# State stores of a two-layer streaming encoder: rows instead of columns, two heads per DMA

## What is computed

```
C_new = decay[..., None, None] * C + jnp.einsum('bhs,bhsd,bhse->bhde', ws, k, v)
n_new = decay[..., None] * n + jnp.einsum('bhs,bhsd->bhd', ws, k)
...
qs = rope(wq.reshape(B, S, SW_HEADS, SW_DH), pos)
ks = rope(wk.reshape(B, S, SW_KV, SW_DH), pos)
new_k, new_v = ks[:, -WINDOW:], vs[:, -WINDOW:]
```

## Time and profile before

| | us |
|---|---|
| median of 3 runs (lowest 2055.12, highest 2057.03) | 2056.2 |
| the profiled execution's own time | 2051.92 |
| its span | 2049.8 |
| TensorE busy in the span | 1999.7 |
| VectorE busy | 1242.4 |
| ScalarE busy | 781.3 |
| GpSimd busy | 945.1 |

### The profile page before, as it was taken

How to read it: one execution, slowest core, us unless ns; L and a number is a source line. 1 busy time by engine, 2 the same in 40 slices (tenths; PEclk the granted TensorE clock), 3 DMA queues, 4 the chain that set the end, 5 groups by cost and what they waited for, 6 DMA issues and landing times.

```text
span 2049.8 us, 39052 instructions
## 1 busy us (share of the span) xinstructions
PE 1999.7 (98%) x15897; PEld 1924.1 (94%) x15897; DVE 1242.4 (61%) x1993; ACT 781.3 (38%) x1672; POOL 945.1 (46%) x532
## 2 busy tenths in 40 slices
PE   8998999999999999999999899999999999999998
PEld 7997898899999999999999889989999999999997
DVE  5564787466647535647567557863765573647473
ACT  4243334223334333425533343342244343525253
POOL 0421244565673646364734212545748446364543
PEclk9998999999999999999999989999999999999999
DMA  9844233123351332323544332332233413232332
GB/s 360 308 135 47 61 104 108 55 73 93 99 188 34 128 126 86 93 83 103 176 167 156 67 55 72 87 104 70 73 93 124 134 46 89 83 91 84 94 93 78
DMA packets 301314, 221.41 MB, mean 108 GB/s; under 512 B 14752, under 2 KB 294864, under 8 KB 297424
## 3 DMA queue, kind: packets, MB, share of 16 engines
q1 hardware_dynamic: 294384, 215.38, 34.9%
q10 hardware_dynamic: 6752, 3.53, 0.7%
HBM read 209.37 MB, written 8.79 MB: 106 GB/s over the span
## 4 chain that ended last, share of the span: by engine, by line
PE 87%; DMA 4%; DVE 3%; POOL 2%; issue 2%; ACT 1%; SPq 0%; DVEq 0%; ACTq 0%; POOLq 0%
PE ps L1196 23%; PE ps L1297 19%; PE ps L1224 14%; PE ps L1664 9%; PE ps L1992 5%; DMA raw<-in_w_in 3%; PE ps L1317 3%; PE ps L1323 2%; PE ps L1450 2%; PE ps L1365 1%; PE ps L1892 1%; PE ps L1855 1%; PE ps L1717 1%; PE ps L1870 1%; PE ps L1732 1%
## 5 line engine op out<-in xcount | busy, mean ns | idle before, releaser
L1123 POOL TENSOR_TENSOR a_lo<-raw,a_hi 128x512 fp32r<-128x512 f32 x108 | 159.3, 1476 | 275.3 <-ACT a_hi L2682 275.3
L1079 POOL TENSOR_TENSOR hi_lo<-raw,consts 128x1024 fp32r<-128x1024 f32 x70 | 141.7, 2025 | 253.5 <-PE ps L1196 153.0
L1196 PE MATMUL ps<-h_hi,hi_lo 128*128 128x288 f32 x1216 | 218.6, 298 | 0.0
L1099 POOL TENSOR_TENSOR hi_lo<-raw,hi_lo 128x512 fp32r<-128x512 f32 x60 | 80.4, 1342 | 292.5 <-ACT hi_lo L2258 292.2
L1196 PEld LDWEIGHTS ps<-h_hi,hi_lo 128*128 128x128 f32 x1216 | 180.0, 189 | 4.4 <-issue 3.2
L1082 POOL TENSOR_TENSOR hi_lo<-raw,hi_lo 128x1024 fp32r<-128x1024 f32 x70 | 177.9, 2541 | 5.5
L1224 PE MATMUL ps<-yf_hi,fo_h 128*128 128x288 f32 x704 | 152.2, 298 | 0.9 <-DVE yf_lo L2857 0.9
L1224 PE MATMUL ps<-yf_hi,fo_l 128*128 128x288 f32 x704 | 150.9, 296 | 0.0
L1224 PE MATMUL ps<-yf_lo,fo_h 128*128 128x288 f32 x704 | 150.8, 296 | 0.0
L1196 PE MATMUL ps<-h_lo,hi_lo 128*128 128x288 f32 x608 | 130.0, 295 | 0.0
L1079 POOL TENSOR_TENSOR hx<-raw,consts 128x1024 fp32r<-128x1024 f32 x28 | 55.6, 1985 | 147.4 <-PE ps L1323 65.0
(11 more groups left out here) (509 smaller groups left out, 6141.4 us busy)
## 6 DMA issues: line engine op xcount, KB each, us to landing
ada<-in_w_ada SPq DMA_DIRECT2D x23, 2048.0 KB, 9.1
raw<-in_w_ffn_in SPq DMA_DIRECT2D x144, 256.0 KB, 3.1
raw<-in_w_in SPq DMA_DIRECT2D x120, 256.0 KB, 3.3
raw<-in_w_in SPq DMA_DIRECT2D x48, 512.0 KB, 3.7
raw<-in_w_ffn_out SPq DMA_DIRECT2D x32, 384.0 KB, 3.3
raw<-in_w_ffn_out SPq DMA_DIRECT2D x32, 320.0 KB, 3.1
raw<-in_w_out SPq DMA_DIRECT2D x16, 512.0 KB, 3.6
raw<-in_w_ffn_in SPq DMA_DIRECT2D x16, 512.0 KB, 3.8
```

What stands on the lines that cost most here:

```text
L1079: pool.tensor_tensor(hi, RAW[s][:, 0:size], ONES[:, 0:1].to_broadcast([128, size]), ALU.mult).then_inc(chunk_hi, 1)
L1099: pool.tensor_tensor(lo, RAWB[o], hi.bitcast(f32), ALU.subtract).then_inc(h_alo, 1)
L1123: pool.tensor_tensor(lo[:, :], RAWB[o], hi[:, :].bitcast(f32), ALU.subtract).then_inc(s_alo, 1)
L1196: m = pe.matmul(o[:, h, :], a[:, k, c0:c0 + 128], mv(k, h), start=(k == 0 and begins), stop=(k == nk - 1 and a is wl))
```

## The change

It has three parts.

**State stores.** `n` is no longer stored as a column. In the turn of head 1, inside `back(0)`, TensorE transposes the 129th columns of the four heads (prompt, then sample: two transposes of 128x4) into free columns of the PSUM unit of `back(0)`, after a wait for head 3's state. In `gate_head(0)` VectorE copies the 4x256 values to `NROWS`, four partitions of the tile KOUT, which is free then, and ScalarE's queue stores them with two DMAs of four rows of 512 bytes (`store_rows`). `C` is stored for two heads by one DMA (`store_states`): heads 0 and 1 where they were, heads 2 and 3 together behind `after_p2(3)`. In all 8 DMAs in place of 18 per layer.

**Order on VectorE.** `rope_sine(1)` stands ahead of `after_p5(8)` (`h_weights(4, 8)` and `h_weights_low(3, 8)`), not behind it.

**Last keys.** The two copies from unit `ko` to KOUT are done by ScalarE, right ahead of the stores, and no longer by VectorE ahead of `after_p7(8)`.

```diff
@@ -322,7 +322,7 @@
 
 
 VROW_DMAS, PARAM_DMAS = 5, 10
-C_STORES, O_STORES = 18, 5
+C_STORES, O_STORES = 8, 5
 
 
 def build(nc, A, O, XD):
@@ -478,6 +478,7 @@
         QK, SU, YTK = MID, MO, KW
         KA, KB = KALL[:, 1, :], KALL[:, 0, :]
         STG, GT = KOUT, SQ
+        NROWS = KOUT[0:4, :, :]
         ADA_BUF = [ADA[:, 0, :], ADA[:, 1, :], ADA2[:, :], ADA3[:, :],
                    MID[:, :, :].rearrange("p k c -> p (k c)")[:, 0:4096]]
         SV = VT[:, :, :, :].rearrange("p t h c -> p (t h c)")[:, 0:2560].rearrange("p (t c) -> p t c", t=5)
@@ -675,7 +676,7 @@
         gh_ready = event("gh_ready", 22)
         gl_ready = event("gl_ready", 22, 2)
         zb_ready = event("zb_ready", 4)
-        c_stored, o_stored, ln_loaded = sem("c_stored"), sem("o_stored"), sem("ln_loaded")
+        c_stored, o_stored, ln_loaded, n_rows = sem("c_stored"), sem("o_stored"), sem("ln_loaded"), sem("n_rows")
 
         def done_by(name):
 
@@ -1743,6 +1744,10 @@
                         pe.wait_ge(unit_of(l, _b(h)[0][0]), read(l, _b(h)[0][0]))
                     for t in range(NTT):
                         pe.transpose(unit(l, nm)[:, t * 128:(t + 1) * 128], YTK[:, t, :], IDN)
+                    if h == 0:
+                        pe.wait_ge(unit_of(l, "cm3"), read(l, "cm3"))
+                        for j in range(2):
+                            pe.transpose(unit(l, nm)[0:4, 640 + j * 128:768 + j * 128], COUT[:, :, j, 128], IDN)
                     pe.transpose(unit(l, nm)[:, 512:576], YTK[0:64, 4, :], IDN[0:64, 0:64]).then_inc(done_by(nm), 1)
 
                 def row_columns():
@@ -2362,13 +2367,17 @@
                     act.dma_start(O[nm][ds(l, 1)].rearrange("l b (h o) -> (l b h) o", o=1), IG[:, c:c + 1]) \
                        .then_inc(c_stored, 16)
 
-                def store_state(h):
-                    act.wait_ge(unit_of(l, f"cm{h}"), read(l, f"cm{h}"))
+                def store_states(h):
+                    act.wait_ge(unit_of(l, f"cm{h + 1}"), read(l, f"cm{h + 1}"))
                     for j, w in enumerate(("prompt", "sample")):
-                        act.dma_start(O[f"C_{w}"][ds(l, 1), 0, h].rearrange("l d e -> (l d) e"), COUT[:, h, j, 0:128]) \
-                           .then_inc(c_stored, 16)
-                        act.dma_start(O[f"n_{w}"][ds(l, 1), 0, h].rearrange("l (d o) -> (l d) o", o=1),
-                                      COUT[:, h, j, 128:129]).then_inc(c_stored, 16)
+                        act.dma_start(O[f"C_{w}"][ds(l, 1), 0, h:h + 2].rearrange("l h d e -> (l d) h e"),
+                                      COUT[:, h:h + 2, j, 0:128]).then_inc(c_stored, 16)
+
+                def store_rows():
+                    act.wait_ge(n_rows, l + 1)
+                    for j, w in enumerate(("prompt", "sample")):
+                        act.dma_start(O[f"n_{w}"][ds(l, 1), 0].rearrange("l h d -> (l h) d"),
+                                      NROWS[:, j, :]).then_inc(c_stored, 16)
 
                 def decay(h):
 
@@ -2406,12 +2415,10 @@
                 after_p5(2)
                 after_p6(2)
                 after_p2(2)
-                store_state(0)
-                store_state(1)
+                store_states(0)
                 after_p7(2)
                 after_p3(2)
                 after_p4(2)
-                store_state(2)
                 for h in range(4):
                     h_keep(0, 3 + h)
                     decay(h)
@@ -2422,7 +2429,9 @@
                     after_p6(3 + h)
                     after_p2(3 + h)
                     if h == 0:
-                        store_state(3)
+                        store_states(2)
+                    elif h == 1:
+                        store_rows()
                     elif h == 2:
                         act.wait_ge(c_stored, l * (16 * C_STORES) + 16 * C_STORES)
                     after_p7(3 + h)
@@ -2449,6 +2458,9 @@
                 after_p5(8)
                 after_p6(8)
                 after_p2(8)
+                act.wait_ge(done_by("ko"), done(l, "ko"))
+                act.activation(KOUT[:, 0, :], unit(l, "ko")[:, 0:128], ACT.Copy)
+                act.activation(KOUT[0:64, 1, :], unit(l, "ko")[0:64, 128:256], ACT.Copy).then_inc(unit_of(l, "ko"), 1)
                 act.wait_ge(unit_of(l, "ko"), read(l, "ko"))
                 for nm, src in (("k_prompt", KOUT[:, 0, :]), ("k_sample", KOUT[0:64, 1, :]),
                                 ("v_prompt", VSW[:, NTT - 1, :]), ("v_sample", VSW[0:64, NTT, :])):
@@ -3394,6 +3406,8 @@
                     nm = _b(h)[1][0]
                     dve.wait_ge(done_by(nm), done(l, nm))
                     h_second_done(dve, l, 2 + h // 2)
+                    if h == 0:
+                        dve.tensor_copy(NROWS, unit(l, nm)[0:4, 640:896].rearrange("p (j c) -> p j c", j=2)).then_inc(n_rows, 1)
                     dve.scalar_tensor_tensor(YT[:, :], MO[:, h, :], 1.0, unit(l, nm)[:, 0:T], ALU.add, ALU.mult).then_inc(unit_of(l, nm), 1)
 
                 def y_lo(i, src):
@@ -3461,13 +3475,10 @@
                 after_p4(7)
                 rope_sum(0)
                 after_p1(8)
+                rope_sine(1)
                 after_p5(8)
-                rope_sine(1)
                 after_p6(8)
                 rope_sum(1)
-                dve.wait_ge(done_by("ko"), done(l, "ko"))
-                dve.tensor_copy(KOUT[:, 0, :], unit(l, "ko")[:, 0:128]).then_inc(dve_step, step())
-                dve.tensor_copy(KOUT[0:64, 1, :], unit(l, "ko")[0:64, 128:256]).then_inc(unit_of(l, "ko"), 1)
                 after_p7(8)
                 after_p3(8)
                 after_p4(8)
```

## The result

The changed kernel takes 2023.26 us (median of 4 runs, 2022.69 to 2023.65) against 2055.66 us before (4 runs, 2054.33 to 2057.03): 32.4 us less, ratio 0.9842 with a 95% interval of 0.9825 to 0.9859. The forecast was 25.2 us less, 2031.0 us, with 2027 as the lower end of its range. The direction and the place were right, the gain was larger than the range allowed. The profiled execution of after took 2023.58 us; that of before had taken 2051.92.

The account below looks back on a forecast made before the run. TensorE, busy 98% of the span, was held by loads slowed behind 4-byte `n` writes. Stop and clock 24.8, minus transposes 0.6, plus rotary part 1.0, gave 25.2 us less: 2031.0 us, range 2027 to 2044.

Parts of the forecast that it names:

- the 7.9 us stop: TensorE's wait at L1697, head 3's state, traced to a load slowed by 4-byte `n` writes; 7.2 us a layer would go.
- Rivals (a) to (c): Load behind head 0/1 stores: `C` shares blame, 2046.6 (0.10); `C` or bank alone, 2055.8 (0.05); pairing `C` slows, 2061.6 (0.03).
- 5.2 us a layer: Time lost to TensorE's half clock from head 3's state to head 0's scores, expected to go with the stop.
- TensorE's new work: Two added transposes of `n` on TensorE, taken as 0.3 us a layer, 0.6 us in all.
- VectorE's copy: Added copy of 4x256 values from PSUM, at most 0.68 us and some 0.4 us, expected to add nothing.
- The two waits of the rotary part: TensorE's 0.5 us for `rope_sine` and 0.7 us for `h_half(8)`; 0.5 us a layer gained together, 1.0 in all.
- the median of the runs stands 4.3 us above that execution, so it would be 2056.2 - 25.2: Step from the profiled execution, 2051.92 us, to the forecast median, 2031.0 us, keeping the offset unchanged.
- I take 3.9 us: Expected duration of the load issued at 156.53 beside 256 KB of `C` rows, instead of 11.14 us.
- The 0.7 us of stop: Part of TensorE's wait at head 3's state expected to stay in each layer, keys being ready at 163.8.
- 24.8 - 0.6: Both layers' gain from stop and clock, 12.4 us each, less the cost of TensorE's added transposes.
- The range: 8 in 10 range for the changed kernel, 2027 to 2044 us; the likeliest case alone spanned 2028 to 2036.
- The two rules: Below 512 bytes a transfer becomes a read-modify-write; or a small packet costs a few cycles and 32 bytes, nearly free.

Follow-up runs that it names:

- `rows_only`: Kernel before with only `n` stored as rows through transposes, `C` still per head and the rotary part as before: 2024.30 us, ratio 0.9854.
- `no_n`: Kernel before with the `n` stores left out, `C` stores as before: 2025.90 us, ratio 0.9846.
- `no_c`: Kernel before with the `C` stores left out, `n` still stored as columns: 2074.51 us, ratio 1.0084.
- `before_again`: Kernel before, unchanged, with clock and span of every run: 2055.02 us over 12 runs.
- `rotary_only`: Kernel before with only `rope_sine(1)` moved earlier and the last keys copied by ScalarE: 2053.36 us, ratio 0.9989.
- `n_step64`: Kernel before with the `n` column elements written 64 bytes apart into the prompt output, `n` itself not stored: 2024.42 us, ratio 0.9863.
- `pairs_only`: Kernel before with only `C` stored in pairs of heads at the change's places, `n` still in 4-byte columns: 2035.04 us, ratio 0.9905.

## Why the prediction was right in the place and wrong in the size

**Right.** The chain's step from the 7.9 us stop to the load behind the stores, and from there to the 4-byte writes, not the `C` rows, carried: `rows_only` and `no_n` get nearly all of the gain. Rivals (a) to (c) are out with them; `no_c` goes further, since it has no `C` rows at all and is slower. One row was misread on the way: the earlier trace rows begins at 193 us, behind the last issue of head 3, and holds about the last of its columns, not its whole store. The reading that the columns take almost no engine time stands even so. The clock went with the stop: 5.2 us a layer had been read for it, and L1698 to the scores is now 13.15 - 7.7 = 5.4 us shorter. TensorE's new work is 0.22 us a layer against 0.3, VectorE's copy 0.41 us and hidden. The two waits of the rotary part went; in their place stand 0.3 + 0.3 us in layer 0 and 0.4 us in layer 1.

**Wrong: the step "the median of the runs stands 4.3 us above that execution, so it would be 2056.2 - 25.2".** It carried over unchanged an offset that was part of what the change removes. After the change the profiled execution, 2023.58 us, and the median, 2023.26, agree. Of the 7.2 us that the forecast gain lacks (32.4 - 25.2), 3.7 (2055.66 - 2051.92) and 0.3 (2023.58 - 2023.26) are this. Behind it is a price set at nothing: slow loads of the next groups were seen, 6.7 to 10.8 us, and passed over because TensorE hardly waited for them in that one execution. In its layer 0 it didn't; in layer 1 it did, for 0.5 us behind a load of 9.05 us, which the prediction, taking layer 1 as a copy of layer 0, did not count. The rows are of before:

```profile
1193.47 9.05 DMA raw<-in_w_in
```

```profile
PE ps L1664 <- DVE hi_lo L2857: 0.5, 1, 0.5
```

By the runs it was a lucky execution: 2051.92 us, where the medians of the five groups are 2051.7 to 2058.2. In others and in kernels with the same writes these loads land up to 5 us later, in `no_c` up to 10, and TensorE stops a second time, at L1745, for 1.7 us (`before_again`), 6.0 (`rotary_only`), 7.9 (`no_c`). The kernel before ran between 2047.5 and 2063.9 us over all its runs, the changed one, with 8 runs, between 2020.0 and 2023.7. That late loads and second stops make up the offset is concluded from these profiles; the execution profiled and the ones timed for the first median are not the same, so it isn't shown for them.

**Mis-sized: "I take 3.9 us" for the load.** It measured 2.9 us, no slower than with nothing in front: 256 KB of `C` rows beside it cost it nothing. The 0.7 us of stop that the sum kept in each layer aren't there: 1.4 us. The rest of the 28.3 us in the profiled times (2051.92 - 2023.58), 1.7 us, can be placed by setting the two traces side by side. From the state to the scores of head 1 layer 0 took 203.57 - 145.21 = 58.36 us before and 192.52 - 147.26 = 45.26 after, 13.1 less; layer 1 took 1211.06 - 1152.14 = 58.92 before and 1183.33 - 1138.07 = 45.26 after, 13.7 less. The first fence is of before, the second of after.

```profile
1152.14 0.89 PE ps L1697 x8
...
1211.06 1.72 PE ps L1717 x6
```

```profile
1138.07 0.89 PE ps L1698 x8
...
1183.33 1.72 PE ps L1718 x6
```

That is 26.8 us, where the sum had 24.8 - 0.6 = 24.2: 1.4 for the stop, 0.4 for the clock (5.4 for 5.2), 0.2 for the transposes and 0.6 for the slower layer 1, most of it the 0.5 us wait above. Over the rotary part the same comparison gives 0.4 and 0.5 us, 0.9 for the 1.0 forecast. Some 0.6 us lie elsewhere. Short falls of the clock to one half play into this: before had two, near 690 and 1130 us, which cost it 1.9 and 1.5 us against after, and after one near 17 us; but after lost 1.9 us in its first 30 us and 1.1 us between 850 and 900 us, so that these nearly cancel. Which short falls come differs between executions of the same kernel. These two rows are of before, the third is of after.

```profile
690.00:694.00 4.00, 3.29 (x15) 3.32 (x16) 3.67 (x7) 1.99 (x5) 0.00 (x0) 0.63 0.43 182
1130.00:1134.00 4.00, 4.00 (x23) 3.98 (x23) 0.60 (x7) 0.37 (x1) 1.27 (x1) 0.67 0.44 118
```

```profile
16.00:20.00 4.00, 4.00 (x62) 3.78 (x66) 1.44 (x9) 2.02 (x4) 0.00 (x0) 0.66 1.19 381
```

**The range** was built from what else could block the load, all on the slow side, down to 2028 for the likeliest case. It had no place for an effect larger in the usual execution than in the profiled one.

**The two rules** of the Trainium skill, page "DMA: Bandwidth & Descriptors": the one in the section "Specifications" pointed the right way, but is too coarse, since being below 512 bytes is not dear by itself here (`n_step64` writes 4 bytes each for nothing, 2024.4 us). The one in "Why small descriptors are slow (HBM only)", by which such packets are nearly free, fits the spread targets (landings of 3.0 us) and fails for neighbours (11 us and more). No run shows a read-modify-write itself.

## What to carry to other kernels

A store whose elements are a few bytes and lie side by side in DRAM (a column of a tile sent to a contiguous vector) is paid by the loads behind it, though it hardly shows in the DMA engines' busy share; turn it into rows on chip, here for 0.6 us of TensorE and VectorE a layer, before looking at how many DMAs there are. When a wait comes from loads that are held up like this, one profile gives one draw of it: price also the late loads that nobody waited for this time, and don't carry a run's offset over an edit that removes its cause. And moving a store by 0.6 us against a load can be worth most of 20 us, as in `pairs_only`, without curing anything.

## What the runs showed of the hardware

- Stores of 128 elements of 4 bytes to one contiguous stretch of 512 bytes, two to four of them within 3 us: a load of 256 KB from DRAM issued 0.25 us behind the first of them lands after 11.1 to 12.9 us, one with two ahead of it after 16.1 and 19.0 us (`no_c`), and later ones after up to 16.6 us, in place of 2.7 to 3.6 us. With the targets 64, 512 or 4096 bytes apart in another tensor, the first load lands after 3.0 to 3.1 us. What happens inside (one element after the other on a shared piece of 64 bytes or less would fit) was not measured; distances between 4 and 64 bytes weren't tried.
- A load issued 0.3 us ahead of the first such store lands after 3.0 and 3.2 us (`pairs_only`), one issued 0.03 us ahead of it after 7.6 us (`rotary_only`).
- The block outlives the stores: in before, nothing moved at 178 to 180 us, some 4 to 6 us behind the last column's issue, and the next loads still crawled.
- Leaving out the stores of 512-byte rows beside such columns made the kernel slower (2074.5 against 2058.2 us); two columns in place of one then went out ahead of the critical load.
- Behind a stop of 7.9 us the granted clock was at one half (1.2 GHz) at 178 to 182 us; behind one of 3.8 us it was at one half too, from 1190 to 1194 us (`pairs_only`, row below). Behind stops of 1.5 us (`pairs_only`, layer 0) and 1.7 us (`before_again`) it stayed at full.

```profile
1190.00:1194.00 4.00, 4.00 (x17) 3.50 (x16) 4.00 (x8) 3.64 (x10) 1.27 (x1) 0.50 0.00 0
```
